# Feed-forward up stage of a two-block transformer kernel: weights as the stationary operand, tokens as the moving one

## The chip, the cores and the metric

The kernel runs on one core of a Trainium2 chip (trn2). The metric is the device time of one execution in microseconds; lower is better. TensorE multiplies (page names PE for matmuls, PEld for the loads of its stationary operand), VectorE (DVE) and ScalarE (ACT) do the elementwise work, SyncE (SP) starts the loads of weights, and GpSimd (POOL) starts a few other transfers. A matmul `matmul(out, lhsT, rhs)` loads `lhsT` into the array (at most 128 x 128) and streams the columns of `rhs` past it (at most 512); the result lands in PSUM, with the columns of `lhsT` as partitions.

## The reference

Two transformer blocks on 256 tokens of width 2048, all in fp32. The part that matters is the feed-forward part at the end of the second block:

```python
h2 = rms_norm_2(x, norm_ffn_pre[l])
up_g, up_v = jnp.split(jnp.einsum('bsd,df->bsf', h2, w_ffn_up[l]), 2, axis=-1)
act = jax.nn.gelu(causal_dwconv3(up_g, conv_ffn_w[l]) + conv_ffn_b[l], approximate=True) * up_v
ffn_out = jnp.einsum('bsf,fd->bsd', act, w_ffn_down[l])
x = x + rms_norm_2(ffn_out, norm_ffn_post[l])

def causal_dwconv3(u, w):          # along the tokens, one weight triple per feature
    return up[:, :s] * w[0] + up[:, 1:s + 1] * w[1] + up[:, 2:] * w[2]
```

`w_ffn_up` is 2048 x 11264 (5632 features of gate, 5632 of value), `w_ffn_down` is 5632 x 2048. The division by the root mean square of a token is one factor per token, and it is applied behind the matmul, to gate and value.

## The kernel before

**One stream of weights.** The program is a sequence of phases (`plan()`), and every phase is a stream of chunks of weights: two k-tiles of 128 rows by 512 columns, 512 KB. SyncE loads a chunk into a ring `raw` of four slots, ScalarE rounds it to fp32r (`hi`), VectorE subtracts to get the rest (`lo = raw - hi`), and TensorE forms each product from three matmuls, `hi*xl`, `hi*xh` and `lo*xh`, where `xh` and `xl` are the same two parts of the activations, already feature-major (features on partitions). ScalarE and VectorE convert three chunks ahead of the one that TensorE is on (`LEAD`); ScalarE's conversion of chunk c + 3 waits until chunk c - 1 has been multiplied, and SyncE's load into a slot waits for `lo` of the chunk that was in it.

**Chunk.** In `chunk()` the activations are the stationary operand: `ah[:, ks, tok]` is 128 features by 128 tokens, and 512 columns of weights stream past. Two k-tiles, two halves of the tokens and three terms make 12 matmuls of 512 columns. The result is token-major (tokens on partitions), 128 x 512 in each of two PSUM banks `acc[pair][t]`. A block of 512 output columns takes eight chunks; gate (block 0, pair 0) and value (block 1, pair 1) of the same 512 features make a pass of 16 chunks.

**Passes.** `ffn_first` is one pass, with the transposes of the activations among its first chunks and the sums for the token factor `rnf` (128 x 2, one column per half of the tokens) in steps 3 to 7; `ffn_up` is a loop of ten; the last pass's elementwise work runs during the first chunks of `ffn_down`. "Step j" of an engine is what it does around chunk j of a pass: VectorE and ScalarE first convert chunk j + 3, then run the side work of the step.

**Side work of a pass, in the next one.** ScalarE evacuates both accumulators with the factor of the token (`ffn_ev`, steps 7 and 15, into `f_g` and `f_v`). TensorE transposes them in groups of four, gate behind chunks 0 and 1, value behind chunks 4 and 5 (`ffn`, into `tp`). VectorE convolves out of PSUM along the tokens (`ffn_conv`, steps 1 and 2, 4 of `tensor_scalar` and 8 of `scalar_tensor_tensor`), ScalarE applies GELU (`ffn_act`, steps 3 and 4), VectorE multiplies by the value (`ffn_mul`, step 6), and the result is split into `fh` and `fl` (`ffn_hi`, `ffn_lo`), the stationary operand of `ffn_down`. The order on each engine is the order in which the code is written; semaphores join the engines (`lo_ready`, `chunk_done`, `acc_free`, and the named steps of a `Stage`).

Of the kernel before, what the change touches and what calls it, by code (L numbers as in the profile page):

```python
# [163 lines left out]
def two_blocks(  # L164
# [152 lines left out]
    f_g = at("f_g", F_W, [T, NB])  # L317
    f_v = at("f_v", F_W + 4096, [T, NB])
# [81 lines left out]
    for n in range(len(LEVELS) + 1):  # L400
# [3 lines left out]
        if n > 0:  # L404
# [9 lines left out]
    ffs = Stage(sem, "ffs", pe=["g0", "g1", "v0", "v1"], act=["ev", "gelu0", "gelu1", "h"],  # L414
                dve=[f"{k}" for c in range(4) for k in (f"c{c}", f"b{c}1", f"b{c}2")] + ["y", "l"])
# [221 lines left out]
    def _(pe):  # L637
# [26 lines left out]
        def stream(side, ready=None):  # L664
            def body(ph, i):
                for j, pos in enumerate(positions(ph)):
                    if ready:
                        ready(i, j)
                    chunk(ph, i, j, pos)
                    side(i, j)  # L670
            return body
# [18 lines left out]
        def stepwise(st, src, ready, side):  # L690
# [12 lines left out]
            return stream(ahead, have)  # L703
# [325 lines left out]
        def ffn_side(i, j):  # L1029
            if j in (0, 1):  # L1030
                ffn(i, j, j)
            if j in (4, 5):
                ffn(i, j, j - 2)

        run(pe, "ffn_first", stepwise(x2_split, lambda t, c: x2[:, t, c:c + P], lambda n: post1.after("dve", f"x{n // 2}"), nothing))
        run(pe, "ffn_up", stream(ffn_side))
        end_phase(pe, "ffn_up", wait=False)

        def down_first(i, j):
            ffn_side(FT // 4 - 1, j)  # L1040
# [4 lines left out]
        run(pe, "ffn_down", stream(nothing), first=stream(down_first, down_ready))  # L1045
# [3 lines left out]
    def _(act):  # L1049
# [447 lines left out]
        def ffn_up(first, ph):  # L1497
            def side(i, j):
                if not first:
                    x2_scales(i, j)  # L1500
                    x2_hi(i, j)
                if first and j in (3, 4):
                    ffn_act(i, j - 3)
                if first and j == 8:
                    ffn_hi(i)
                if j == 7:
                    ffn_ev(i, 0, ph)
                if j == 15:
                    ffn_ev(i, 1, ph)
                    act.drain().then_inc(*ffs.mark("act", "ev"))  # L1510
            return side

        def ffn_act(i, h):
            act.wait_ge(*ffs.after("dve", f"b{2 * h + 1}2", i))
# [9 lines left out]
        run(act, "ffn_first", stream(ffn_up(0, phases["ffn_first"])))  # L1524
        act.wait_ge(out_x2, 16)
        run(act, "ffn_up", stream(ffn_up(1, phases["ffn_up"])))
# [4 lines left out]
        def down_first(i, j):  # L1531
            if j in (3, 4):
                ffn_act(FT // 4 - 1, j - 3)
            if j == 8:
# [12 lines left out]
    def _(dve):  # L1547
# [545 lines left out]
        def ffn_conv(i, h):  # L2093

            dve.wait_ge(*ffs.after("pe", f"g{h}", i))
            for c in (2 * h, 2 * h + 1):
                w = lambda k: vcol[:, V_FW[k][0], bass.ds(i * 4 + (V_FW[k][1] + c), 1)]
                u = tp[h][:, (c % 2) * S:(c % 2 + 1) * S]
                v.tensor_scalar(f_c[:, c], u, w(2), None, ALU.mult).then_inc(*ffs.mark("dve", f"c{c}"))
                dve.wait_ge(*ffs.after("dve", f"c{c}", i))  # L2100
                for back in (1, 2):
                    v.scalar_tensor_tensor(f_c[:, c, back:S], u[:, 0:S - back], w(2 - back), f_c[:, c, back:S],
                                           ALU.mult, ALU.add).then_inc(*ffs.mark("dve", f"b{c}{back}"))
                    dve.wait_ge(*ffs.after("dve", f"b{c}{back}", i))

        def ffn_mul(i):
            dve.wait_ge(*ffs.after("act", "gelu1", i))
# [6 lines left out]
        def ffn_lo(i):  # L2114
            dve.wait_ge(*ffs.after("act", "h", i))
            k = bass.ds(i * 4, 4)
# [16 lines left out]
        def down_side(i, j):  # L2133
            if i == 0:
                ffn_side(FT // 4 - 1, j)
# [31 lines left out]
```

## Time and profile before

| | us |
|---|---|
| median of 3 runs (lowest to highest) | 2629.25 (2628.07 to 2629.6) |
| span of the profiled execution | 2625.2 |
| TensorE, matmuls | 2575.0 busy |
| TensorE, weight loads | 2123.9 busy |
| VectorE | 1482.2 busy |
| ScalarE | 1372.7 busy |
| up stage, one pass of `ffn_up` | 45.45 |

The span of the profiled execution is 4.05 us shorter than the median of the runs. A matmul's record begins when it starts and ends when its results are modelled to have landed, so records overlap: what a stream costs is read from start to start. `acc<-hi,xl` reads as: written to `acc`, moving operand `hi`, stationary operand `xl`; a weight load has the name of its matmul. In a form such as 128*12 128x256 the stationary operand has 12 columns and the moving one 256. The granted clock is 1.00 at 2.4 GHz and 0.50 at 1.2 GHz.

### The profile page before, as it was taken

To read this page: it belongs to the slowest core of one execution; us is meant where nothing else is said; L and a number is where in the kernel's file an instruction comes from. 1 tells how busy PE (TensorE), PEld (TensorE's weight loads), DVE (VectorE), ACT (ScalarE), POOL (GpSimd) and SP (SyncE) were. 2 spreads that over 40 slices of the span, in tenths; PEclk is the share of its full clock that TensorE was granted. 3 is DMA by queue.
4 is the path that set the end of the run, shared out by engine and by line. 5 is a ranking of instruction groups with operands and counts; after the bars stand their busy time and mean duration, and the time that the engine had idled before them with its cause. 6 is when DMAs were issued, how large, how long until landed. Compare 5 with 4: busy or idle time off the path is not lost.

```text
span 2625.2 us, 34962 instructions
## 1 busy us (share of the span) xinstructions
PE 2575.0 (98%) x11926; PEld 2123.9 (81%) x11926; DVE 1482.2 (56%) x1959; ACT 1372.7 (52%) x1925; POOL 9.0 (0%) x17
## 2 busy tenths in 40 slices
PE   7999999999999999999999999999999999999998
PEld 6788788788878888888888888878788888888886
DVE  4455555555556544445477776555556565665444
ACT  5454655555445544454576665444555455554443
POOL 0000000000000000000000000000000000000000
PEclk9999999999999999999999999999999999999999
DMA  7555565556665666655555555666556656566564
GB/s 259 166 162 168 152 193 164 156 173 179 209 215 181 212 192 192 192 169 176 160 161 169 166 169 163 192 198 218 183 179 190 189 178 192 169 198 221 196 198 148
DMA packets 242763, 482.18 MB, mean 184 GB/s; under 512 B 15138, under 2 KB 15440, under 8 KB 240496
## 3 DMA queue, kind: packets, MB, share of 16 engines
q1 hardware_dynamic: 240240, 462.52, 57.7%
q0 software_dynamic: 2432, 18.46, 2.0%
q8 instruction: 56, 0.92, 0.1%
q14 instruction: 35, 0.29, 0.0%
HBM read 474.62 MB, written 6.30 MB: 183 GB/s over the span
## 4 chain that ended last, share of the span: by engine, by line
PE 96%; ACT 2%; DVE 1%; issue 1%; DMA 0%; DVEq 0%; ACTq 0%; SPq 0%
PE acc L639 89%; PE sc L639 3%; PE tp L643 3%; ACT L1051 0%; ACT hi L1051 0%; DVE lo L1552 0%; DMA x_in<-in_x 0%; DVE x2b L2070 0%; ACT sc L1051 0%; PE sc L643 0%; DVE ssh L1722 0%; ACT b_sq L1051 0%; DVE ol L1575 0%; DVE xl L1573 0%; DVE mem_in L1597 0%
## 5 line engine op out<-in xcount | busy, mean ns | idle before, releaser
L1552 DVE TENSOR_TENSOR lo<-raw,hi 128x1024 fp32r<-128x1024 f32 (+1 forms) x896 | 1066.5, 1195 | 940.1 <-ACT hi L1051 932.0
L1051 ACT ACTIVATE hi<-raw 128x1024 fp32r<-128x1024 f32 (+1 forms) x896 | 924.1, 1036 | 845.6 <-PE acc L639 793.9
L639 PE MATMUL acc<-hi,xl 128*128 128x512 f32 x2368 | 946.8, 400 | 9.5 <-DVE lo L1552 5.3
L639 PE MATMUL acc<-lo,xh 128*128 128x512 f32 x2368 | 926.6, 391 | 0.0
L639 PE MATMUL acc<-hi,xh 128*128 128x512 f32 x2368 | 924.6, 390 | 0.0
L639 PEld LDWEIGHTS acc<-hi,xl 128*128 128x128 f32 x2368 | 446.5, 189 | 106.3 <-issue 13.4
L639 PEld LDWEIGHTS acc<-lo,xh 128*128 128x128 f32 x2368 | 445.9, 188 | 96.4
L639 PEld LDWEIGHTS acc<-hi,xh 128*128 128x128 f32 x2368 | 446.9, 189 | 87.5
L639 PE MATMUL acc<-hi,ol 128*128 128x512 f32 x640 | 256.8, 401 | 5.5 <-DVE ol L1575 5.5
L639 PE MATMUL acc<-lo,oh 128*128 128x512 f32 x640 | 250.5, 391 | 0.0
L639 PE MATMUL acc<-hi,oh 128*128 128x512 f32 x640 | 249.8, 390 | 0.0
L639 PEld LDWEIGHTS acc<-hi,ol 128*128 128x128 f32 x640 | 120.7, 189 | 28.8 <-DVE ol L1575 6.0
L639 PEld LDWEIGHTS acc<-lo,oh 128*128 128x128 f32 x640 | 120.4, 188 | 26.4
L639 PEld LDWEIGHTS acc<-hi,oh 128*128 128x128 f32 x640 | 120.9, 189 | 23.2
L639 PE MATMUL acc<-hi,fl 128*128 128x512 f32 x352 | 137.4, 390 | 0.3 <-issue 0.3
L639 PE MATMUL acc<-lo,fh 128*128 128x512 f32 x352 | 137.0, 389 | 0.0
L639 PE MATMUL acc<-hi,fh 128*128 128x512 f32 x352 | 137.0, 389 | 0.0
L1051 ACT ACT_TABLE_LOAD x85 | 109.1, 1283 | 31.7 <-PE tp L643 10.8
L639 PEld LDWEIGHTS acc<-hi,fl 128*128 128x128 f32 x352 | 66.1, 188 | 14.3 <-issue 0.7
L639 PEld LDWEIGHTS acc<-lo,fh 128*128 128x128 f32 x352 | 66.1, 188 | 13.9
L639 PEld LDWEIGHTS acc<-hi,fh 128*128 128x128 f32 x352 | 66.1, 188 | 13.5
L639 PE MATMUL acc<-hi,m2l 128*128 128x512 f32 x128 | 50.7, 396 | 0.3 <-issue 0.3
(301 smaller groups left out, 1478.5 us busy)
## 6 DMA issues: line engine op xcount, KB each, us to landing
raw<-in_w_in SPq DMA_DIRECT2D x416, 512.0 KB, 3.9
raw<-in_w_ffn_up SPq DMA_DIRECT2D x176, 512.0 KB, 4.4
raw<-in_w_ffn_down SPq DMA_DIRECT2D x80, 512.0 KB, 4.7
raw<-in_w_out SPq DMA_DIRECT2D x64, 512.0 KB, 4.4
raw<-in_w_mem_kv SPq DMA_DIRECT2D x48, 512.0 KB, 4.0
raw<-in_w_branch SPq DMA_DIRECT2D x48, 512.0 KB, 4.1
raw<-in_w_branch_a SPq DMA_DIRECT2D x8, 512.0 KB, 4.8
raw<-in_w_branch_b SPq DMA_DIRECT2D x8, 512.0 KB, 4.8
```

Of the source, the lines that this page charges most:

```text
L639: return nc.tensor.matmul(o, lhsT, rhs, start=start, stop=stop)
L643: return nc.tensor.transpose(o, in_, ident[0:k, :])
L1051: return nc.scalar.activation(o, in_, func, **kw)
L1552: v.tensor_tensor(lo[:, slot, 0:size], raw[:, slot, 0:size], hi[:, slot, 0:size].bitcast(F32), ALU.subtract).then_inc(lo_ready, 1)
```

## The change

In `ffn_first` and `ffn_up`, TensorE runs a new `chunk_by_feature`: 128 columns of weights are the stationary operand, all 256 tokens the moving one. Gate and value land feature-major, as the convolution and `ffn_down` want them, and the transposes go. The token factor is then a factor per column: VectorE makes two diagonal matrices from `rnf`, TensorE multiplies them by a matrix of ones, and the result, `f_r`, holds the factor of every token on every partition. VectorE reads the accumulators itself: `ffn_gate` scales the gate from PSUM in step 8 of the same pass, the convolution follows in steps 9 and 10, GELU in 10 and 11, `ffn_scale` multiplies the GELU by the value's factor in step 12, and `ffn_mul` multiplies by the value from PSUM in step 0 of the next pass. ScalarE's `ffn_ev` goes.

```diff
-    f_g = at("f_g", F_W, [T, NB])
-    f_v = at("f_v", F_W + 4096, [T, NB])
+    f_g = at("f_g", F_W, [4, S])
+    f_r = at("f_r", F_W + 4096, [S])
+    f_diag = at("f_diag", F_W + 5120, [T, P])
...
+        def chunk_by_feature(ph, i, j, pos):
...
+            for kk in range(size):
+                ks = place(k0 + kk)
+                for m in range(4):
+                    feat = slice(m * P, (m + 1) * P)
+                    o = acc[pair][m // 2][:, (m % 2) * S:(m % 2 + 1) * S]
+                    end = last and kk == size - 1
+                    opens = k0 + kk == 0 and m % 2 == 0
+                    nc.tensor.matmul(o, hi[:, slot, kk, feat], al[:, ks], start=opens, stop=False, skip_group_check=True)
+                    nc.tensor.matmul(o, hi[:, slot, kk, feat], ah[:, ks], start=False, stop=False, skip_group_check=True)
+                    ins = nc.tensor.matmul(o, lo[:, slot, kk, feat], ah[:, ks], start=False, stop=end, skip_group_check=True)
+            ins.then_inc(chunk_done, 1)
...
-        def ffn(i, at_, step):
-
-            st, n = ("g", f_g) if step < 2 else ("v", f_v)
-            h = step % 2
-            pe.wait_ge(*ffs.after("act", "ev", i))
-            if step >= 2:
-                pe.wait_ge(*ffs.after("dve", f"b{2 * h + 1}2", i))
-            for c in range(2):
+        def first_side(i, j):
+            if j == 8:
+                pe.wait_ge(*ffr.after("dve", "d"))
                 for t in range(T):
-                    ins = tr(tp[h][:, c * S + t * P:c * S + (t + 1) * P], n[:, t, (2 * h + c) * P:(2 * h + c + 1) * P])
-            ins.then_inc(*ffs.mark("pe", f"{st}{h}"))
...
+                    ins = mm(sc[1][:, t * P:(t + 1) * P], kc[:, K_ONE:K_ONE + P], f_diag[:, t])
+                ins.then_inc(*ffr.mark("pe", "r"))
...
-        run(pe, "ffn_up", stream(ffn_side))
+        run(pe, "ffn_up", stream(nothing, one=chunk_by_feature))
...
-        def ffn_ev(i, blk, ph):
-
-            act.wait_ge(chunk_done, ph.chunk(i, KT // 2 * (blk + 1) - 1) + 1)
-            for t in range(T):
-                go((f_g, f_v)[blk][:, t], acc[blk][t][:], ACT.Identity, scale=rnf[:, t:t + 1]).then_inc(acc_free[blk], 1)
...
+        def ffn_side(i, j):
+            if j == 1:
+                ffn_hi(i)
+            if j in (10, 11):
+                ffn_act(i + 1, j - 10)
...
+            if j == 7:
+                dve.wait_ge(*x2_norm.after("dve", "r"))
+                for t in range(T):
+                    ins = v.tensor_scalar(f_diag[:, t], ident, rnf[:, t:t + 1], None, ALU.mult)
+                ins.then_inc(*ffr.mark("dve", "d"))
...
+        def ffn_gate(ph, i, it):
+
+            dve.wait_ge(chunk_done, ph.chunk(i, KT // 2 - 1) + 1)
             for h in range(2):
-                dve.wait_ge(*ffs.after("pe", f"v{h}", i))
+                v.tensor_tensor(f_g[:, 2 * h:2 * h + 2], acc[0][h][:].rearrange("p (a b) -> p a b", a=2), by_token(2),
+                                ALU.mult).then_inc(acc_free[0], 1)
+            dve.drain().then_inc(*ffs.mark("dve", "g0"))
+            dve.wait_ge(*ffs.after("dve", "g0", it))
...
+        def ffn_scale(it):
+            dve.wait_ge(*ffs.after("act", "gelu1", it))
+            v.tensor_tensor(f_a[:], f_a[:], by_token(4), ALU.mult).then_inc(*ffs.mark("dve", "s"))
...
+        def ffn_mul(before, it):
+
+            dve.wait_ge(chunk_done, before + 1)
+            dve.wait_ge(*ffs.after("dve", "s", it))
+            for h in range(2):
                 part = f_a[:, 2 * h:2 * h + 2].rearrange("p a b -> p (a b)")
-                ins = v.tensor_tensor(part, part, tp[h][:], ALU.mult)
-            ins.then_inc(*ffs.mark("dve", "y"))
...
+                v.tensor_tensor(part, part, acc[1][h][:], ALU.mult).then_inc(acc_free[1], 1)
+            dve.drain().then_inc(*ffs.mark("dve", "y"))
...
         def ffn_side(i, j):
-            if j in (1, 2):
-                ffn_conv(i, j - 1)
-            if j == 6:
-                ffn_mul(i)
-            if j == 9:
+            ph = phases["ffn_up"]
+            if j == 0:
+                ffn_mul(ph.chunk(i, -1), i)
+            if j == 2:
                 ffn_lo(i)
+            if j == 8:
+                ffn_gate(ph, i, i + 1)
+            if j in (9, 10):
+                ffn_conv(i + 1, j - 9)
+            if j == 12:
+                ffn_scale(i + 1)
```

In the loop's body TensorE's queue had 208 matmuls (192 and 16 transposes) and now has 384; each is an entry for the weight load and one for the matmul, and with registers and the branch that makes 438 instructions before and 787 after.

TensorE before, in the loop of the up stage, the end of chunk 0 and the first group of transposes (`kc` holds the identity):

```order
L639 MATMUL acc00<-hi_50,xh_52 128x512
L639 MATMUL acc00<-lo_51,xh_52 128x512
L639 MATMUL acc01<-hi_50,xl_53 128x512
L639 MATMUL acc01<-hi_50,xh_52 128x512
L639 MATMUL acc01<-lo_51,xh_52 128x512
L1021 ISA
L643 MATMUL tp0<-kc_60,f_g_157 128x128 x4
```

TensorE after, in the same chunk, a k-tile's four groups of three, two per PSUM bank:

```order
L683 MATMUL acc01<-xh_52,hi_50 128x256
L684 MATMUL acc01<-xh_52,lo_51 128x256
L682 MATMUL acc00<-xl_53,hi_50 128x256
L683 MATMUL acc00<-xh_52,hi_50 128x256
L684 MATMUL acc00<-xh_52,lo_51 128x256
L682 MATMUL acc00<-xl_53,hi_50 128x256
L683 MATMUL acc00<-xh_52,hi_50 128x256
```

The transposes behind the chunk are gone, each matmul has half the columns, and operands have changed sides: the first name behind the arrow is the moving one.

VectorE before, the start of side work in step 1 of the loop, behind the `lo` of that step:

```order
L1552 TENSOR_TENSOR lo<-raw,hi 128x1024
L2095 ISA
L2099 ISA
L2099 TENSOR_SCALAR f_c<-tp,vcol 128x256
L2100 ISA
L2102 ISA
L2102 SCALAR_TENSOR_TENSOR f_c<-tp,vcol,f_c 128x255
```

VectorE after, steps 8 and 9 of the loop:

```order
L1550 TENSOR_TENSOR lo<-raw,hi 128x1024
L2112 TENSOR_TENSOR f_g<-acc,f_r 128x512 x2
L2115 ISA
L1549 REGISTER_ALU
L1550 TENSOR_TENSOR lo<-raw,hi 128x1024
L2122 ISA
L2122 TENSOR_SCALAR f_c<-f_g,vcol 128x256
```

The convolution has moved from steps 1 and 2 of the next pass to steps 9 and 10 of the same one, reads `f_g` in SBUF instead of `tp` in PSUM, and has the scaling out of the accumulators ahead of it.

## Rows read from the trace of the kernel before

**Rows 1.** The page: busy time by engine, and the chain that ended last
```profile
PE 2575.0 (98%) x11926; PEld 2123.9 (81%) x11926; DVE 1482.2 (56%) x1959; ACT 1372.7 (52%) x1925; POOL 9.0 (0%) x17
...
PE 96%; ACT 2%; DVE 1%; issue 1%; DMA 0%; DVEq 0%; ACTq 0%; SPq 0%
PE acc L639 89%; PE sc L639 3%; PE tp L643 3%; ACT L1051 0%; ACT hi L1051 0%; DVE lo L1552 0%; DMA x_in<-in_x 0%; DVE x2b L2070 0%; ACT sc L1051 0%; PE sc L643 0%; DVE ssh L1722 0%; ACT b_sq L1051 0%; DVE ol L1575 0%; DVE xl L1573 0%; DVE mem_in L1597 0%
```
**Rows 2.** One pass: length; busy of PE, PEld, DVE, ACT, POOL; clock, DMA share, GB/s
```profile
1957.45:2002.90 45.45, 45.45 (x210) 37.60 (x209) 27.29 (x32) 24.29 (x27) 0.00 (x0) 1.00 0.61 185
```
**Rows 3.** Groups of instructions, 1912 to 2366: count, busy us, mean ns, idle before, releasers
```profile
L1552 DVE TENSOR_TENSOR lo<-raw,hi 128x1024 fp32r<-128x1024 f32 x160 | 193.4, 1224 | 165.7 <-ACT hi L1051 162.8
L1051 ACT ACTIVATE hi<-raw 128x1024 fp32r<-128x1024 f32 x160 | 168.3, 1058 | 155.3 <-PE acc L639 155.2
...
L2102 DVE SCALAR_TENSOR_TENSOR f_c<-tp,vcol,f_c 128x255 f32<-128x255 f32 x80 | 38.6, 482 | 12.9 <-DVE f_c L2099 2.7 <-DVE f_c L2102 0.2
...
L1051 ACT ACTIVATE f_a<-f_c,vcol 128x256 f32<-128x256 f32 x40 | 18.2, 502 | 17.6 <-DVE f_c L2102 17.5
L2111 DVE TENSOR_TENSOR f_a<-f_a,tp 128x512 f32<-128x512 f32 x20 | 12.8, 681 | 0.0
...
L2117 DVE TENSOR_TENSOR fl<-f_a,fh 128x1024 f32 x10 | 12.2, 1219 | 0.0
```
**Rows 4.** TensorE in order of time, chunk 8 of ffn_first: start us, us, instruction
```profile
1894.06 0.39 PE L639 MATMUL acc<-hi,xl 128*128 128x512 f32 x1
...
1896.78 0.39 PE L639 MATMUL acc<-hi,xl 128*128 128x512 f32 x1
```
**Rows 5.** Tiles `f_g` and `f_v`: ns min/median/max, first and last start us
```profile
L643 PE MATMUL tp<-kc,f_g x88: 270/272/273, 1918.5 to 2377.2; 128*128 128x128 f32 x88
L1051 ACT ACTIVATE f_g<-acc,rnf x22: 681/686/690, 1894.3 to 2349.4; 128x512 f32<-128x512 f32 x22
...
L643 PE MATMUL tp<-kc,f_v x88: 270/272/273, 1930.4 to 2389.0; 128*128 128x128 f32 x88
```
**Rows 6.** TensorE in order of time, around a group of transposes
```profile
1918.31 0.39 PE L639 MATMUL acc<-lo,xh 128*128 128x512 f32 x1
1918.54 0.60 PE L643 MATMUL tp<-kc,f_g 128*128 128x128 f32 x4
...
1919.21 0.40 PE L639 MATMUL acc<-hi,xh 128*128 128x512 f32 x1
...
1919.91 0.39 PE L639 MATMUL acc<-hi,xh 128*128 128x512 f32 x1
```
**Rows 7.** Tile `rnf` in `ffn_first`, its last write
```profile
L1613 DVE RECIPROCAL rnf<-rnf x1: 158/158/158, 1894.1 to 1894.1; 128x2 f32<-128x2 f32 x1
```
**Rows 8.** TensorE: 256 fp32r columns past 12 columns of weights; last, their window
```profile
270.13 0.28 PE L639 MATMUL sc<-xh,wf_lo 128*12 128x256 f32 x1
...
271.88 0.28 PE L639 MATMUL sc<-xh,wf_lo 128*12 128x256 f32 x1
...
275.39 0.28 PE L639 MATMUL sc<-xh,wf_hi 128*12 128x256 f32 x1
...
271.90:275.40 3.50, 3.50 (x34) 2.81 (x32) 1.23 (x1) 1.43 (x5) 0.00 (x0) 1.00 0.79 187
```
**Rows 9.** Weight loads in order of time, merged, ahead of fp32 matmuls of 128 and 256 columns
```profile
544.24 0.86 PEld L639 LDWEIGHTS sc<-mk,c_pt 128*128 128x128 f32 x7
...
1152.83 1.48 PEld L639 LDWEIGHTS sc<-d_kt,d_qt 128*128 128x128 f32 x7
```
**Rows 10.** ScalarE and VectorE in order of time, conversion of one chunk
```profile
1996.04 1.06 ACT L1051 ACTIVATE hi<-raw 128x1024 fp32r<-128x1024 f32 x1 [1.66 <-PE acc L639]
...
1997.14 1.23 DVE L1552 TENSOR_TENSOR lo<-raw,hi 128x1024 fp32r<-128x1024 f32 x1 [1.49 <-ACT hi L1051]
```
**Rows 11.** DMA queues (packets, MB, share): 1912 to 1957 first, then 1957.5 to 2366
```profile
q1 hardware_dynamic: 4335, 8.35, 59.4%
q8 instruction: 2, 0.03, 0.3%
...
q1 hardware_dynamic: 39124, 75.42, 60.4%
...
raw<-in_w_ffn_up SPq DMA_DIRECT2D x139, 512.0 KB, 4.4
```

More of the change, by code:

```diff
@@ L413, in two_blocks @@
     post1 = Stage(sem, "post1", act=["rt"], dve=["w0", "w1", "w2", "ms", "e", "w3", "r", "x0", "x1", "x2", "x3"])
[L414 to L415 removed]
+    ffr = Stage(sem, "ffr", pe=["r"], dve=["d", "r"])
+    ffs = Stage(sem, "ffs", act=["gelu0", "gelu1", "h"],
+                dve=["g0"] + [f"{k}{h}" for h in range(2) for k in ("c", "b", "d")] + ["s", "y", "l"])
     post2 = Stage(sem, "post2", act=["rt"], dve=["w0", "w1", "w2", "ms", "e", "w3", "r", "x0", "x1", "x2", "x3"])
@@ L662, in chunk, with stream @@
             ins.then_inc(chunk_done, 1)
-        def stream(side, ready=None):
+        def chunk_by_feature(ph, i, j, pos):
+            blk, k0, size, last = pos
+            pair = blk % 2
+            slot = (ph.c0 + j) % RING
+            ah, al, place = stationary(ph.name, blk)
+            if k0 == 0 and not (isinstance(i, int) and ph.use(i, blk) == 0):
+                pe.wait_ge(acc_free[pair], 2 * ph.use(i, blk))
+            pe.wait_ge(lo_ready, ph.chunk(i, j) + 1)
+            for kk in range(size):
[9 more added lines that the diff above has]
+            ins.then_inc(chunk_done, 1)
+        def stream(side, ready=None, one=chunk):
             def body(ph, i):
@@ L668, in body @@
                         ready(i, j)
-                    chunk(ph, i, j, pos)
+                    one(ph, i, j, pos)
                     side(i, j)
@@ L688, in norm_split, with stepwise @@
             split(st, src, st.after("dve", "n1"), n)
-        def stepwise(st, src, ready, side):
+        def stepwise(st, src, ready, side, one=chunk):
             for n in range(2):
@@ L702, in have @@
                     pe.wait_ge(*st.after("dve", f"l{j}"))
-            return stream(ahead, have)
+            return stream(ahead, have, one)
         pe.wait_ge(in_first, 16 * 2)
@@ L1044, in down_ready @@
                 pe.wait_ge(*ffs.after("dve", "l", FT // 4 - 1))
-        run(pe, "ffn_down", stream(nothing), first=stream(down_first, down_ready))
+        run(pe, "ffn_down", stream(nothing), first=stream(nothing, down_ready))
     @block_ctx.scalar
@@ L1489, in _, with first_side @@
         end_phase(act, "out_2", wait=False)
-        def ffn_ev(i, blk, ph):
-            act.wait_ge(chunk_done, ph.chunk(i, KT // 2 * (blk + 1) - 1) + 1)
-            for t in range(T):
-                go((f_g, f_v)[blk][:, t], acc[blk][t][:], ACT.Identity, scale=rnf[:, t:t + 1]).then_inc(acc_free[blk], 1)
[L1497 to L1511, printed above, removed]
+        def first_side(i, j):
+            x2_scales(i, j)
+            x2_hi(i, j)
+            if j in (11, 12):
+                ffn_act(0, j - 11)
+        def ffn_side(i, j):
[3 more added lines that the diff above has]
+                ffn_act(i + 1, j - 10)
         def ffn_act(i, h):
-            act.wait_ge(*ffs.after("dve", f"b{2 * h + 1}2", i))
+            act.wait_ge(*ffs.after("dve", f"d{h}", i))
             for c in (2 * h, 2 * h + 1):
@@ L1521, in ffn_hi @@
             go(fh[:, bass.ds(i * 4, 4)], f_a[:]).then_inc(*ffs.mark("act", "h"))
-        run(act, "ffn_first", stream(ffn_up(0, phases["ffn_first"])))
+        run(act, "ffn_first", stream(first_side))
         act.wait_ge(out_x2, 16)
-        run(act, "ffn_up", stream(ffn_up(1, phases["ffn_up"])))
+        run(act, "ffn_up", stream(ffn_side))
         end_phase(act, "ffn_up")
@@ L2091, in first_side @@
             x2_scales(i, j)
[L2093 to L2104, printed above, removed]
@@ new lines, in first_side, with by_token @@
+            if j == 9:
+                dve.wait_ge(*ffr.after("pe", "r"))
+                v.tensor_copy(f_r[:], sc[1][:, 0:S]).then_inc(*ffr.mark("dve", "r"))
+                dve.wait_ge(*ffr.after("dve", "r"))
+                ffn_gate(phases["ffn_first"], 0, 0)
+            if j in (10, 11):
+                ffn_conv(0, j - 10)
+            if j == 13:
+                ffn_scale(0)
+        def by_token(n):
+            return f_r[:].unsqueeze(1).to_broadcast([P, n, S])
+        def ffn_gate(ph, i, it):
+            dve.wait_ge(chunk_done, ph.chunk(i, KT // 2 - 1) + 1)
+            for h in range(2):
+                v.tensor_tensor(f_g[:, 2 * h:2 * h + 2], acc[0][h][:].rearrange("p (a b) -> p a b", a=2), by_token(2),
+                                ALU.mult).then_inc(acc_free[0], 1)
+            dve.drain().then_inc(*ffs.mark("dve", "g0"))
+            dve.wait_ge(*ffs.after("dve", "g0", it))
@@ new lines, in ffn_conv @@
+        def ffn_conv(it, h):
+            w = lambda c, k: vcol[:, V_FW[k][0], bass.ds(it * 4 + (V_FW[k][1] + c), 1)]
+            two = (2 * h, 2 * h + 1)
+            for c in two:
+                ins = v.tensor_scalar(f_c[:, c], f_g[:, c], w(c, 2), None, ALU.mult)
+            ins.then_inc(*ffs.mark("dve", f"c{h}"))
+            for back, was, step in ((1, "c", "b"), (2, "b", "d")):
+                dve.wait_ge(*ffs.after("dve", f"{was}{h}", it))
+                for c in two:
+                    ins = v.scalar_tensor_tensor(f_c[:, c, back:S], f_g[:, c, 0:S - back], w(c, 2 - back), f_c[:, c, back:S],
+                                                 ALU.mult, ALU.add)
+                ins.then_inc(*ffs.mark("dve", f"{step}{h}"))
@@ L2133, in down_side @@
         def down_side(i, j):
-            if i == 0:
-                ffn_side(FT // 4 - 1, j)
+            if (i, j) == (0, 0):
+                ffn_mul(ph.chunk(0, -1), FT // 4 - 1)
+            if (i, j) == (0, 2):
+                ffn_lo(FT // 4 - 1)
             if (i, j) in ((0, 26), (1, 2), (1, 26)):
```

22 lines of the change are left out of this document (6 added, 16 removed).

## The prediction, made before the changed kernel ran

> **What bounds the kernel now.** I read the page first: TensorE is busy 98% of the span and carries 96% of the chain that ended last, almost all of it matmuls into `acc` [rows 1]. So only what shortens or lengthens TensorE's stream counts, or what makes it wait. Then one pass of the up stage: in 45.45 us TensorE is busy for all of them at a granted clock of 1.00, the 2.4 GHz level, while VectorE works 27.3 us and ScalarE 24.3 us [rows 2]. Both have idle time ahead of their work on weights: in ten passes VectorE waits 165.7 us ahead of `lo` for ScalarE, and ScalarE 155.3 us ahead of `hi` for TensorE [rows 3]. TensorE is the bound, and its helpers have slack.
>
> **What a clean chunk costs.** In a stretch without transposes, from the matmul at 1894.06 to the one at 1896.78, 12 matmuls of 512 columns take 2.72 us, 226.7 ns from start to start [rows 4]. The 390 ns of a single one is latency, which the next one overlaps. A pass has 16 chunks of 12, so 192 x 0.2267 = 43.52 us. The pass takes 45.45 us: from the first evacuation of gates at 1894.3 to the last at 2349.4, second of its pair and so 0.6 late, ten passes go by in 454.5 us [rows 5].
>
> **What the change removes on TensorE.** 88 transposes of `f_g` and as many of `f_v`, in groups of four, 4 groups in each of 11 passes [rows 5]. Read one group: the last matmul ahead of it starts at 1918.31, the second behind it at 1919.21, so 0.90 us hold two matmuls' worth of stream (0.453) and 0.445 us that are the group's [rows 6]. The three steps from 1919.21 to 1919.91 are slower than clean ones by 0.02 us together. Four groups make 1.9 us, and 45.45 - 43.52 = 1.93 us says the same from the other side. All of it lies on the path: 11 x 1.93 = **21.2 us gained**.
>
> **What it adds on TensorE.** Two fp32 matmuls for the row `f_r`, once. Plain fp32 is run as two passes, so four entries of the kind of a transpose group: 0.5 us. They wait for `f_diag`, made by VectorE in step 7. `rnf` is final at 1894.1 + 0.16, and TensorE asks for the diagonals behind chunk 8, at 1896.78 [rows 4, 7]. Two small operations fit in 2.5 us, so I take no wait.
>
> **What it exchanges, the term that decides.** Each matmul of 512 columns becomes two of 256, with the weights as stationary operand: 384 instead of 192 in a pass, and as many weight loads. The columns streamed are the same. A weight load must now hide behind 256 columns, and the trace has no 256-column fp32r matmul with a full 128-column load. I bound one by four neighbours:
> - 256 fp32r columns with a load of 12 columns: from 271.88 to 275.39 are 31 steps, 113.3 ns each, and the clock is at 1.00 there [rows 8]. That is half of 226.7 to a tenth of a nanosecond. Since the 512-column matmul had a load of 128 columns and this one of 12, neither the number of instructions nor the size of the load shows in the time. Sum by it: no change.
> - Loads of 128 columns back to back behind short fp32 matmuls: seven loads in 0.86 us, the last 0.19 long, so (0.86 - 0.19)/6 = 112 ns from one to the next [rows 9]. A full load is done in 112 ns, just under 113.3.
> - fp32 matmuls of 256 columns in two passes, 512 half-steps each: (1.48 - 0.19)/6 = 215 ns for a computed 213.3 [rows 9]. Full loads hide entirely behind them; some 2 ns could be a fixed part of each matmul.
> - The first 15 steps of the 256-column row, from 270.13 to 271.88, took 117 ns each [rows 8]. I do not know why.
>
> Least is 0 (the same columns cannot stream faster than the row), and most, if the whole 13.4 ns above 213.3 in a 512-column step belonged to the instruction, is 106.7 + 13.4 = 120 ns. I take 113.3, because the nearest row by data type and width has it and the load fits by 1 ns. **Exchange: 0, bounds 0 to 4224 x 6.7 ns = +28 us**, 4224 being 11 x 384.
>
> The Trainium skill, TensorE: Matmul & The Clock Gate, section Back-to-back issue gap, speaks against the change: warm matmuls are N/2.4 plus about 2.5 ns apart, so a split costs 2.5 ns each time. By that the 2112 additional matmuls would cost 5.3 us and the sum would be 5.3 us worse. The fp32 rows agree with such a part, the fp32r rows at 113.3 and 226.7 do not.
>
> **What moves on VectorE and ScalarE.** ScalarE loses four evacuations of 0.69 us per pass [rows 5], and by the order of instructions the loads of an activation table too. VectorE gets two products from PSUM, like the 0.68 us of `f_a<-f_a,tp`, and one of 1024 columns, like the 1.22 us of `fl`: 2.6 us more, 29.9 of 43.5 [rows 3]. The busy time is harmless; the order needs a look, because the next `lo` stands behind each wait. Chunk c's `lo` is due 3 chunks (8.16 us) after the start of chunk c-3; normally it is ready 2.3 us after it (`hi` 1996.04, `lo` done 1998.37) [rows 10]. The waits for `acc` in steps 0 and 8 come behind a `lo` whose `hi` itself waited for the same chunk, so they cost nothing. The convolution of steps 9 and 10 is 12 operations; I take 0.48 us for each, as eight of them took before [rows 3]. `lo` of step 9 ends at 2.4 us into chunk 9, the first half at 5.4, `lo` of step 10 at 6.6, the second half at 9.6, two more `lo` by 12.1. The last of them, of chunk 15, is then 12.1 - 3 x 2.72 = 3.9 us into chunk 12 if only VectorE is counted; its `hi` stands behind the second GELU on ScalarE (9.6 + 1.0 + 1.1 = 11.7, so `lo` at 12.9, 4.8 us into chunk 12) [rows 3]. Due is 8.16. Cover: over 3 us. Without it each further microsecond per pass costs 11. A `raw` slot falls free with that `lo` and is filled in a median 4.4 us [rows 11]: 9.2 us into chunk 12, which is before its own `hi` at 10.9. I cost these edits at nothing.
>
> **Sum.** 2625.2 - 21.2 + 0.5 = 2604.5 us by the profiled execution. The median of the runs is 4.05 us above that span, so **2608.5 us**, 0.8% faster. It breaks even at 113.3 + 20.7 us/4224 = 118.2 ns a step.
>
> **Rivals.**
> - *A fixed part in each matmul.* 2.1 ns, as the fp32 rows allow: 2112 x 2.1 = 4.4 us, **2613 us**. For it: rows 9. Against it: rows 8. The skill's rule of 2.5 ns above is this rival, a microsecond worse.
> - *The weight load shows through.* 112 ns is so near to 113.3 that a handshake or two reads of SBUF at once could set the pace. At the 117 ns of the first steps in rows 8: 4224 x 3.6 ns = 15 us, **2624 us**. For it: those steps, and that the load is now hidden by nothing but 1 ns. Against it: the 31 steps behind them.
> - *Slower: the excess belongs to the load, not to the columns.* 120 ns a step costs 28 us: **2637 us**. It decides from 118.2 ns on. For it: every fp32r matmul with a 128-column load is 13.4 ns over its 512/2.4. Against it: the 12-column rows pay exactly half of it for half the columns.
> - *Slower: the loop no longer stays with the engine.* The body grows from 438 to 787 instructions on TensorE's queue. In the first pass two pieces of code of 16 KB are fetched, and in the nine that follow none [rows 11]. So 438 instructions, touching three pieces of 256, are kept across the branch. If 787 are not, each of 9 branches waits up to a transfer's 4.4 us: up to 40 us, **2648 us** at most. The Trainium skill, Runtime: NRT & Kernel Launch, section Instruction fetch mechanics, says that a taken branch to code outside a two-page window stalls for the fetch. By that rule the loop before would have fetched too, and rows 11 show that it did not; the same section gives TensorE room for 2048 instructions, which no run here shows.
> - *A new wait.* VectorE's convolution takes over 3 us longer than reckoned and TensorE waits at chunk 15. The gain is gone at 1.9 us per pass: **about 2620 to 2630 us**.
>
> **How the numbers follow.** Forecast (no change in the exchange) 0.50; fixed part 0.15; load shows through (115 to 118 ns) 0.13; load pays 120 ns 0.12; loop not kept 0.05; new wait 0.05. The range runs from 2604, since the runs of before spread over 1.5 us and what a removed group trails behind it may reach further than I counted, to 2627, which takes in the first three cases and the mild half of a new wait: 0.80. A measurement of this kernel tells 0.2% (5.3 us) from no change. Faster by more (under 2624.0): 0.50 + 0.15 + 0.11 + 0.02 = 0.78. Within it: 0.02 + 0.02 + 0.01 = 0.05. Slower: 0.17.
>
> **What would show it.** One pass of the up stage at 43.5 us and TensorE without idle time in it; steps of 113 ns between 256-column matmuls, 112 or less from load to load where they queue; clock 1.00; no instruction packets between the first pass and the last; `lo` of chunk 15 ready 3 us early. It is wrong if the steps are 117 ns or more, if weight loads lie end to end with matmuls behind them, or if TensorE idles before chunk 0, 15 or 16 of a pass.

## The result, and the profile after

The changed kernel takes 2633.9 us in the median of 19 runs (2629.74 to 2636.69), beside 2629.14 for the kernel before in the median of as many (2623.64 to 2630.69). The ratio is 1.0023, with a 95% interval of 1.0016 to 1.0030. A second comparison gave 2633.34 against 2627.01, 1.0030 [1.0018, 1.0042]. So the kernel got slower, by 0.2 to 0.3%, where 0.8% faster was forecast, and the time lies 7 us above the end of the range.

The page of the changed kernel, its busy times, the chain, and two of the new groups:

```profile
PE 2579.6 (98%) x13866; PEld 2217.2 (84%) x13866; DVE 1497.3 (57%) x1995; ACT 1324.2 (50%) x1862; POOL 9.0 (0%) x17
...
PE 96%; ACT 2%; DVE 1%; issue 1%; DMA 0%; DVEq 0%; ACTq 0%; SPq 0%
...
L682 PE MATMUL acc<-xl,hi 128*128 128x256 f32 x1408 | 400.3, 284 | 1.0 <-DVE xl L1571 1.0
...
L682 PEld LDWEIGHTS acc<-xl,hi 128*128 128x128 f32 x1408 | 271.4, 193 | 1.4 <-DVE xl L1571 1.4
```

TensorE has 1940 more matmuls (13866 against 11926 in [rows 1]): 2112 from the split and 4 for the row `f_r`, less 176 transposes. It is still the bound, with the same 98% and 96%. The only new names in the chain are those of the new matmuls.

One pass of the up stage, in the columns of [rows 2], an interval between two taken branches of the loop:

```profile
2006.20:2052.28 46.08, 46.08 (x386) 46.08 (x386) 28.57 (x34) 19.49 (x22) 0.00 (x0) 1.00 0.62 182
```

It is 46.08 us, where 45.45 stood before and 43.5 was forecast. The clock is 1.00, so nothing was lost there. What is new is the third number: the weight loads fill the whole pass (before 37.60 of 45.45), as the prediction listed among its signs of being wrong. A load's record is 192 ns long and the next load starts 120 ns behind it, so this number alone doesn't say that the loads set the pace. TensorE in order of time, inside that stage:

```profile
1998.22 0.28 PE L684 MATMUL acc<-xh,lo 128*128 128x256 f32 x1
1998.34 0.28 PE L682 MATMUL acc<-xl,hi 128*128 128x256 f32 x1
1998.46 0.28 PE L683 MATMUL acc<-xh,hi 128*128 128x256 f32 x1
1998.58 0.28 PE L684 MATMUL acc<-xh,lo 128*128 128x256 f32 x1
```

Each step is 0.12 us. From 2004 to 2054 us 416 matmuls start, each 120 ns behind the one before it, to the nanosecond, where 113.3 was forecast. 384 x 0.120 = 46.08: the step accounts for the pass, and there is no other time in it. What the pass gained by losing its transposes (1.93 us) is less than what 384 steps lost (384 x 6.7 ns = 2.56 us), and the difference of 0.63 us comes 11 times, 6.9 us. The eleventh time is `ffn_first`, whose matmuls are slower too, against the transposes that are gone from the start of `ffn_down`. The matmuls for `f_r` add 0.44 us once. The two profiled spans differ by 4.4 us, not by 7.3. Of the other 2.9 us, 2.5 arose before the changed stage, since TensorE starts its first matmul in `ffn_first` at 1863.99 us here and at 1866.45 in the kernel before. The rest is in the first six chunks of `ffn_first`.

All the waits that the profile of the changed kernel shows from 1960 to 2370 us (who waited for what, us in total, times, longest us):

```profile
ACT hi L1061 <- PE acc L684: 211.1, 125, 1.8
DVE lo L1550 <- ACT hi L1061: 151.0, 116, 1.7
ACT f_a L1061 <- DVE f_c L2127: 26.4, 18, 1.8
```

TensorE is not among those that wait. The loss is therefore in the pace of its own stream.

### The profile page after: what moved, and what is told of

It reads as the page before. It is cut to its first block, busy times and chain, and to the rows that moved or that the text cites. A ratio compares the mean times of both kernels' runs of the same rounds, so it can differ in the third digit from the quotient of the medians.

```text
span 2629.6 us, 38693 instructions
## 1 busy us (share of the span) xinstructions
PE 2579.6 (98%) x13866; PEld 2217.2 (84%) x13866; DVE 1497.3 (57%) x1995; ACT 1324.2 (50%) x1862; POOL 9.0 (0%) x17
## 4 chain that ended last, share of the span: by engine, by line
PE 96%; ACT 2%; DVE 1%; issue 1%; DMA 0%; DVEq 0%; ACTq 0%; SPq 0%
PE acc L641 71%; PE acc L682 6%; PE acc L684 6%; PE acc L683 6%; PE sc L641 3%; PE tp L645 2%; ACT L1061 0%; ACT hi L1061 0%; DVE lo L1550 0%; DMA x_in<-in_x 0%; DVE x2b L2068 0%; ACT sc L1061 0%; PE sc L645 0%; DVE ssh L1720 0%; ACT b_sq L1061 0%
## 5 line engine op out<-in xcount | busy, mean ns | idle before, releaser
L641 PE MATMUL acc<-hi,xl 128*128 128x512 f32 x1664 | 666.7, 401 | 8.5 <-DVE lo L1550 5.3
L641 PE MATMUL acc<-lo,xh 128*128 128x512 f32 x1664 | 650.6, 391 | 0.0
L641 PE MATMUL acc<-hi,xh 128*128 128x512 f32 x1664 | 649.2, 390 | 0.0
L682 PE MATMUL acc<-xl,hi 128*128 128x256 f32 x1408 | 400.3, 284 | 1.0 <-DVE xl L1571 1.0
L684 PE MATMUL acc<-xh,lo 128*128 128x256 f32 x1408 | 399.5, 284 | 0.0
L683 PE MATMUL acc<-xh,hi 128*128 128x256 f32 x1408 | 399.5, 284 | 0.0
L641 PEld LDWEIGHTS acc<-hi,xh 128*128 128x128 f32 x1664 | 313.9, 189 | 60.8
L682 PEld LDWEIGHTS acc<-xl,hi 128*128 128x128 f32 x1408 | 271.4, 193 | 1.4 <-DVE xl L1571 1.4
L683 PEld LDWEIGHTS acc<-xh,hi 128*128 128x128 f32 x1408 | 271.4, 193 | 0.0
L684 PEld LDWEIGHTS acc<-xh,lo 128*128 128x128 f32 x1408 | 271.4, 193 | 0.0
```

Of the source, the lines that this page charges most:

```text
L641: return nc.tensor.matmul(o, lhsT, rhs, start=start, stop=stop)
L682: nc.tensor.matmul(o, hi[:, slot, kk, feat], al[:, ks], start=opens, stop=False, skip_group_check=True)
L683: nc.tensor.matmul(o, hi[:, slot, kk, feat], ah[:, ks], start=False, stop=False, skip_group_check=True)
L684: ins = nc.tensor.matmul(o, lo[:, slot, kk, feat], ah[:, ks], start=False, stop=end, skip_group_check=True)
```

## The experiments

The order is that of what they decide: first the two halves of the change apart, then the disputed step by itself, then versions that use what was learned.

**The transposes gone, the matmuls as before.** The changed kernel with token-major matmuls of 512 columns in both up stages:

```diff
-                                       first_side, chunk_by_feature))
-        run(pe, "ffn_up", stream(nothing, one=chunk_by_feature))
+                                       first_side))
+        run(pe, "ffn_up", stream(nothing))
```

> The changed kernel with its elementwise work and without transposes, but the up stage multiplied as before (activations stationary, 512 columns of weights moving), so what lands in the accumulators is token-major and the output is not the reference's. It is the removal alone. If the transposes' cost was read rightly, a pass takes 43.5 us instead of 45.45 and the time is 21 us under the kernel before: ratio 0.992. If the new work on VectorE delays TensorE, or the transposes were partly hidden, less than that.

Measured: 2607.15 us beside 2626.94, ratio 0.9921 [0.9905, 0.9938]. That is 20.8 us gained by the ratio, 19.8 between the medians. Its pass:

```profile
2005.00:2048.52 43.52, 43.52 (x194) 36.05 (x193) 28.57 (x34) 19.55 (x22) 0.00 (x0) 1.00 0.62 192
```

43.52 us is 192 x 226.7 ns and nothing beside it. The new work of VectorE and ScalarE is all in this kernel, and it costs nothing. The term of 21.2 us for the removal holds: ten passes are 1.93 us shorter each.

**The split alone.** The kernel before, transposes and all, with `chunk_by_feature` put in for its matmuls:

```diff
-        run(pe, "ffn_up", stream(ffn_side))
+        run(pe, "ffn_up", stream(ffn_side, one=chunk_by_feature))
```

and the same in `ffn_first`.

> The kernel before, with the up stage's matmuls exchanged for the 256-column ones (weights stationary) and everything else left, transposes and evacuations too; gate and value are then in the wrong layout, so the output is not the reference's. It is the exchange alone. At 120 ns a step instead of 113.3: 11 passes x 384 x 6.7 ns = 28 us slower, ratio 1.011. If the 120 ns came from something else in the changed kernel (VectorE reading the accumulators, for one), the steps here are 113.3 ns and the ratio is 1.000.

Measured: 2653.59 us beside 2626.94, ratio 1.0102 [1.0085, 1.0119]. That is 26.8 us lost by the ratio, 26.7 between the medians. TensorE in order of time:

```profile
1999.77 0.28 PE L682 MATMUL acc<-xh,lo 128*128 128x256 f32 x1
1999.89 0.28 PE L680 MATMUL acc<-xl,hi 128*128 128x256 f32 x1
2000.01 0.28 PE L681 MATMUL acc<-xh,hi 128*128 128x256 f32 x1
```

Again 120 ns, without VectorE reading the accumulators. The two halves, -20.8 and +26.8 by their ratios, add up to +6.0 us. The change as a whole costs 6.0 and 7.9 us by the ratios of its two comparisons, 4.8 and 6.3 between the medians. So the failing term is the exchange, and the other terms are right. What remained was why a step takes 120 ns, since two rivals (the load shows through; a fixed part in each matmul) and the slower one (the excess belongs to the load) could all be stretched to it.

**The step by itself.** A kernel of its own with groups of 48 matmuls in a row, each group with one shape and one PSUM bank, stationary tiles taken in turn, and nothing else running:

```diff
+        for k in range(N): mm(ps[1][:, 0:384], wr[k % 2][:, 0:128], xr[:, 0:384], start=True, stop=True)
+        for k in range(N): mm(ps[3][:, 0:256], wr[k % 2][:, 0:128], xr[:, 0:256], start=True, stop=True)
+        for k in range(N): mm(ps[3][0:12, 0:256], wr[k % 2][:, 0:12], xr[:, 0:256], start=True, stop=True)
```

> No part of the reference: groups of 48 matmuls, stationary operand of m columns, moving one of n, one after the other on an idle chip. Theory A: each weight load of 128 columns costs the stream 13.3 ns whatever streams behind it, one of 12 columns 6.7 ns. Then m=128: n=512 227, 384 173.3, 320 146.7, 256 120, and 192 and 128 at the load's own pace, about 112; m=12: 256 113.3, 512 220; pairs of 512 and 256: 347. Theory B: columns of fp32r stream at 16/17 of the clock, and a load behind such a stream takes 120 ns. Then m=128: n=384 170, 320 141.7, 256, 192 and 128 all 120; m=12: 256 113.3, 512 226.7; m=64, n=256 113.3. fp32 of 256 columns is 215 in both; bfloat16 is not in the trace: A says 227 and 120 again.

TensorE in order of time, each group merged into one row (start, length of the whole group, shapes of load and matmul, count):

```profile
27.97 11.04 PE L59 MATMUL ps<-xr,wr 128*128 128x512 f32 x48
38.85 8.51 PE L60 MATMUL ps<-xr,wr 128*128 128x384 f32 x48
47.20 7.19 PE L61 MATMUL ps<-xr,wr 128*128 128x320 f32 x48
54.23 5.92 PE L62 MATMUL ps<-xr,wr 128*128 128x256 f32 x48
...
65.74 5.50 PE L64 MATMUL ps<-xr,wr 128*128 128x192 f32 x48
71.08 5.50 PE L65 MATMUL ps<-xr,wr 128*128 128x128 f32 x48
...
98.36 5.60 PE L69 MATMUL ps<-xr,wr 128*12 128x256 f32 x48
103.80 11.26 PE L70 MATMUL ps<-xr,wr 128*12 128x512 f32 x48
114.90 20.88 PE L71 MATMUL ps<-xf,wf 128*128 128x256 f32 x96
...
156.69 5.40 PE L74 MATMUL ps<-xb,wb 128*128 128x256 bf16 x48
```

A group's length less its last matmul's duration, over 47, is the step: for 256 columns (5.92 - 0.28)/47 = 120.0 ns. In the same way 512 columns give 226.7, 384 give 173.3, 320 give 146.7. (Where the first few steps of a group are uneven, the number is that of the settled ones behind them; for 384 columns the whole group would give 173.9.) The granted clock is 1.00 throughout. Taking away columns / 2.4 leaves 13.3 ns **every time**, at 256 as at 512, as long as the load has 128 columns. At 192 and at 128 columns the step stays at 111.7: there the load sets the pace, and the 112 ns from [rows 9] was right. The same stationary tile each time instead of two in turn (the next row of that kernel) gives 120.0 as well. The row with a load of 12 columns, on which the forecast rested, is there too: 113.3, and loads of 32 and 64 columns give the same to half a nanosecond. But 12 columns of load with 512 of matmul take 231 ns, more than a full load does, so a small load isn't simply cheaper.

Other data types have a far smaller fixed part. bf16 takes 109.2 ns for 256 columns (and 215.8 for 512, 55.8 for 128), where 106.7 are the columns alone. The 48 fp32 matmuls of 256 columns are 96 entries in the row above, and each entry takes 215.8 ns, 2.5 more than twice its 256 columns. By the Trainium skill, TensorE: Matmul & The Clock Gate, section Back-to-back issue gap, steps of N columns are N/2.4 plus about 2.5 ns. The trace agrees with that for bf16. It doesn't for fp32r, which has 13.3, and an fp32 entry has the 2.5 only over twice its columns.

Of the two theories on record the full-load rows fit the first, 13.3 ns for each load of 128 columns. It missed bf16 (227 and 120 expected) and the 12-column load behind 512 columns (220 expected). Every matmul here has a load of its own, so a fixed part in each matmul and one in each load look the same until the load's size changes.

**Loads of other sizes.** At 256 columns the full load gave 120.0 and small ones 113.3. If the size of the load were the cause, the step should follow it. The same kernel with other shapes:

```diff
+        for k in range(N): mm(ps[1][0:112, 0:256], wr[k % 2][:, 0:112], xr[:, 0:256], start=True, stop=True)
+        for k in range(N): mm(ps[3][0:80, 0:256], wr[k % 2][:, 0:80], xr[:, 0:256], start=True, stop=True)
+        for k in range(N): mm(ps[2][0:12, 0:384], wr[k % 2][:, 0:12], xr[:, 0:384], start=True, stop=True)
```

> No part of the reference: groups of 48 matmuls of fp32r, stationary operand of m columns, moving one of n. From the first table the price of a load is 13.3 ns for 128 columns and 6.7 for 64, 32 and 12, when n is 256. If it goes by started halves of 64 columns, m=72 to 112 cost 13.3 (120 ns at n=256) and 64 costs 6.7; if in proportion, 96 columns cost 10 to 12. At n=384 and 320: m=128 13.3 over the columns; m=64, 32, 12: 166.7 and 140 if the price is the load's, else the erratic 230 of n=512 shows here too. Pairs of 512 and 256 in separate banks: 347. 64 rows instead of 128 at m=128, n=256: 120 if the price goes by columns of weights, less if by bytes of the whole load.

```profile
27.66 5.92 PE L59 MATMUL ps<-xr,wr 128*128 128x256 f32 x48
33.41 5.61 PE L60 MATMUL ps<-xr,wr 128*112 128x256 f32 x48
38.85 5.73 PE L61 MATMUL ps<-xr,wr 128*96 128x256 f32 x48
44.42 5.62 PE L62 MATMUL ps<-xr,wr 128*80 128x256 f32 x48
...
69.32 8.48 PE L66 MATMUL ps<-xr,wr 128*64 128x384 f32 x48
...
85.97 8.54 PE L68 MATMUL ps<-xr,wr 128*12 128x384 f32 x48
```

Loads of 112, 96, 80, 72 and 64 columns give steps of 113.4, 116.1, 113.3, 116.7 and 113.4 ns. There is no order among them, neither the halves nor the proportion that was expected, but all lie below the 120.0 of the full load. At 384 columns a smaller load saves nothing: 175.0 for 96 columns of load, 173.4 for 64, 173.3 for 32, 175.0 for 12, beside 173.3 for a full one. So "the excess belongs to the load" is no rule for all widths. At 256 columns, the width of the changed kernel, 3.3 to 6.7 of the 13.3 ns do go with the full load in this kernel.

**Widths around 256.** The same again in steps of 16 columns, with full loads and with loads of 12:

```diff
+        for k in range(N): mm(ps[4][0:128, 0:272], wr[k % 2][:, 0:128], xr[:, 0:272], start=True, stop=True)
+        for k in range(N): mm(ps[5][0:12, 0:256], wr[k % 2][:, 0:12], xr[:, 0:256], start=True, stop=True)
+        for k in range(N): mm(ps[6][0:12, 0:272], wr[k % 2][:, 0:12], xr[:, 0:272], start=True, stop=True)
```

> No part of the reference: groups of 48 fp32r matmuls, m columns stationary, n moving. Theory C, by the tables so far: steps come in units of 6.67 ns (16 columns), a stream pays one or two units over its own, and a full load, whose own pace is 111.7 ns, just misses the 113.3 that 256 columns would take. Then m=128: n=208 to 240 about 111.7 to 113.3, 256 120, 272 120 to 126.7, the same as m=12 from 272 or 288 on; m=120 or 124 at n=256: between 113.3 and 120. Theory A (a price on each full load) wants m=128 over m=12 by 6.7 ns at every n. Runs: 512 and 256 by turns 353 a pair, in runs of 2, 4, 8 falling to 346.7.

| columns | 208 | 224 | 240 | 256 | 272 | 288 | 304 | 320 |
|---|---|---|---|---|---|---|---|---|
| columns / 2.4, ns | 86.7 | 93.3 | 100.0 | 106.7 | 113.3 | 120.0 | 126.7 | 133.3 |
| step, load of 128 | 111.6 | 111.6 | 111.7 | 120.0 | 125.3 | 131.7 | 137.7 | 146.7 |
| step, load of 12 | | | 111.1 | 117.8 | 124.4 | 131.2 | 140.0 | 146.7 |

```profile
43.74 5.91 PE L62 MATMUL ps<-xr,wr 128*128 128x256 f32 x48
49.49 6.18 PE L63 MATMUL ps<-xr,wr 128*128 128x272 f32 x48
...
75.48 5.80 PE L67 MATMUL ps<-xr,wr 128*120 128x256 f32 x48
81.12 5.91 PE L68 MATMUL ps<-xr,wr 128*124 128x256 f32 x48
...
98.23 5.81 PE L71 MATMUL ps<-xr,wr 128*12 128x256 f32 x48
103.88 6.14 PE L72 MATMUL ps<-xr,wr 128*12 128x272 f32 x48
```

From 256 columns on, a step in this kernel is the columns and 11 to 13.3 ns, with either load. At 272 the small load costs what the full one does, to a nanosecond. The load of 12 columns with 256 took 117.8 ns here and 113.3 in the first kernel of steps, for the same shape. So the row that the forecast took as its nearest neighbour stands for one width, and it isn't even stable there; [rows 8] shows both of its paces, 117 ns for the first 15 steps and 113.3 for the 31 behind them.

At 256 columns the two rows above add the loads between 112 and 128 columns: 117.3 ns for 120 columns and 120.0 for 124. That is where the theory on record put them, by which a full load, at its own pace of 111.7, just misses the 113.3 that the columns would take. What isn't separated is how much of the 120 ns at 256 columns is the fixed part and how much the load: by the kernel before this one the load's share is up to 6.7 ns, by this one, against the 12-column load, 2.2. With the full load of the changed kernel all three kernels give 120.0, and the price doesn't depend on the answer.

**Fewer, wider matmuls, feature-major.** If each fp32r matmul with a full load pays 13.3 ns, the changed kernel can win some back by joining two of the three terms: `hi` meets `xh` and `xl`, both with the same stationary tile, so one matmul of 512 columns can do for two of 256. Its two halves land side by side in a whole PSUM bank (the four banks of `acc` and `sc` or `tp` take a chunk's four feature tiles), `lo` times `xh` is added to the second half, ScalarE copies the first half out, and VectorE adds the second to it. Only the loop `ffn_up` is changed so; `ffn_first` stays as in the changed kernel:

```diff
+                for m in range(4):
...
+                    if ks == 0:
+                        nc.tensor.matmul(wide[pair][m][:], hi[:, slot, kk, feat], both, start=True, stop=False, skip_group_check=True)
+                    ins = nc.tensor.matmul(wide[pair][m][:, S:], lo[:, slot, kk, feat], xh[:, ks], start=False, stop=False, skip_group_check=True)
+                    if ks:
+                        ins = nc.tensor.matmul(wide[pair][m][:], hi[:, slot, kk, feat], both, start=False, stop=end, skip_group_check=True)
```

> The changed kernel, and in ffn_up the two terms that share a stationary operand, hi*xh and hi*xl, are one matmul of 512 columns into a whole bank; lo*xh stays at 256 columns, ScalarE copies one half of each bank and VectorE adds the other. 256 loads in a pass instead of 384, the same columns. If each full load costs 13.3 ns of stream (theory A), a pass takes 128 x (226.7 + 120) = 44.4 us, against 46.1 changed and 45.45 before: 17 us under the changed kernel, 12 us under the one before, ratio 0.995. If the price belongs to columns (theory B) and 120 ns is a floor of the load, the sum is the same 44.4, so this run does not tell the theories apart; it tells whether fewer loads pay in the kernel. If the extra work (3 us a pass on VectorE, 1.5 us on ScalarE) delays TensorE, less.

Measured: 2624.93 us beside 2627.01, ratio 0.9992 [0.9983, 1.0001], level with the kernel before. Its pass:

```profile
2005.56:2050.77 45.21, 45.21 (x259) 39.24 (x257) 31.07 (x41) 21.59 (x29) 0.00 (x0) 1.00 0.63 186
```

The direction is right, 0.87 us less than the changed kernel's 46.08. But a pair of 512 and 256 columns takes 353.2 ns (45.21 us / 128), 6.5 more than 226.7 + 120.0, and the pass misses the 44.4 us expected. TensorE has no wait in it, so the extra work of the other engines isn't what delays it.

**The same, equal widths in runs.** In each k-tile four matmuls of one width and then four of the other, with the order reversed from one k-tile to the next, so that up to eight of a width stand in a row:

```diff
+                for term in ("hi", "lo") if ks % 2 == 0 else ("lo", "hi"):
+                    for m in range(4):
```

> e4 with the order of matmuls changed: eight of 512 columns in a row, then eight of 256, instead of one by one. In e4 a pair took 353 ns instead of 346.7, and in the second table a mixture of widths was as uneven. If the turn from one width to the other costs, runs of eight bring the pair near 346.7 and a pass from 45.2 to 44.4 or 44.5 us: 7 us under e4, ratio 0.996 to the kernel before. If the 353 belong to the joined operand or to the bank written, nothing changes: 0.999.

Measured: 2620.83 us beside 2626.8, ratio 0.9974 [0.9963, 0.9984]. Its pass:

```profile
2004.72:2049.41 44.69, 44.69 (x258) 39.33 (x257) 31.00 (x41) 21.59 (x29) 0.00 (x0) 1.00 0.64 188
```

A pair takes 349.1 ns now (44.69 / 128), still 2.4 over the sum. This one beats both kernels: by its ratio 6.8 us under the one before (6.0 between the medians), and by the ratios 13 to 15 us under the changed one, whose ratios are 1.0023 and 1.0030. The traces say the same: ten passes at 44.69 instead of 45.45 are 7.6 us, less 1.1 us for what stays as in the changed kernel (`ffn_first` 2.56 slower, `f_r` 0.44, and the last pass's transposes, 1.93, gone from the start of `ffn_down`).

**The changed kernel again**, beside the first joined one:

> The changed kernel itself, beside the others on the same chip: 4 to 7 us over the kernel before, ratio 1.0023 as measured first.

Measured: 2633.34 us, ratio 1.0030, told above.

## Why the prediction was wrong, step by step

- **What bounds the kernel, and a clean chunk:** right. TensorE has no idle time in the up stage before or after, and without transposes a pass is 43.52 us, as computed.
- **What is removed, 21.2 us:** right, 20.8 measured by the ratio and 19.8 between the medians.
- **What is added, 0.5 us for `f_r`:** right. The diagonals are made at 1892.5 us and used at 1895.2, so there is no wait, and chunk 8 of `ffn_first` with them is 0.44 us longer than its neighbours.
- **What it exchanges: 0 was taken, it was +28 us by the steps** (4224 x 6.7 ns) and 26.8 by the run of the split alone, where a pass with its transposes takes 47.81 us: 46.08 and 1.73 for the transposes, which cost 0.2 less there. This is the step that failed. The forecast set 113.3 ns (a load of 12 columns, 256 of matmul) beside 226.7 (load of 128, 512 of matmul), saw exactly half, and concluded that the 13.3 ns over 512/2.4 are proportional to the columns. That changed two sizes between two rows and read a law out of their ratio. With the full load kept, the 13.3 ns are the same at 256, 320, 384 and 512 columns, so halving the columns pays them twice. The coincidence came from the one width where a smaller load is cheaper: 113.3 is found at 256 columns alone, with loads of up to 112 columns, and not in every program. The upper bound, "if the whole 13.4 ns belonged to the instruction, 120 ns", was the truth; it got 0.12 of the chance because the coincidence to a tenth of a nanosecond looked like evidence.
- **A fixed part in each matmul:** the mechanism that fits every row with a full load, with the wrong size. It was sized at 2.1 ns from plain fp32 matmuls in [rows 9], and another data type didn't carry over: fp32r has 13.3. The 2.5 ns that the prediction took from the Trainium skill would have been off in the same way.
- **The weight load shows through, 117 ns:** its number for the load's own pace was right (111.7), and from 208 to 240 columns the step is the load's. At 256 the step is 8.3 ns above that pace, so the load alone doesn't account for it; that it has a share of up to 6.7 ns isn't excluded, as the rows with smaller loads show.
- **The excess belongs to the load, 2637 us:** its price of 120 ns a step was the measured one. As a mechanism it fails from 272 columns on, where a smaller load saves at most 1 ns, and at 512 columns it costs 3 to 4 more. At 256 it can hold for half of the 13.3 ns and not for all of them.
- **The loop no longer stays with the engine:** didn't happen. DMA queues of the changed kernel (packets, MB, share), 1912 to 1960 us first, then 1960 to 2374:

```profile
q1 hardware_dynamic: 4610, 8.89, 62.7%
q8 instruction: 3, 0.05, 0.4%
...
q1 hardware_dynamic: 39060, 75.30, 62.3%
```

Three pieces of code come in the first pass and none in the nine that follow, whose window has no row for an instruction queue, so 787 instructions are kept across the branch. The Trainium skill, Runtime: NRT & Kernel Launch, section Instruction fetch mechanics, has a taken branch out of a two-page window stall for a fetch. The trace doesn't show that: the matmuls run on at 120 ns across the branch.
- **A new wait on VectorE:** didn't happen, with more room than reckoned. VectorE in order of time:

```profile
2033.53 1.28 DVE L2112 TENSOR_TENSOR f_g<-acc,f_r 128x512 f32<-128x512 f32 x2
2035.27 1.23 DVE L1550 TENSOR_TENSOR lo<-raw,hi 128x1024 fp32r<-128x1024 f32 x1 [0.46 <-ACT hi L1061]
2036.41 0.61 DVE L2122 TENSOR_SCALAR f_c<-f_g,vcol 128x256 f32<-128x256 f32 x2
2037.16 1.90 DVE L2127 SCALAR_TENSOR_TENSOR f_c<-f_g,vcol,f_c 128x255 f32<-128x255 f32 x4
...
2044.80 1.23 DVE L1550 TENSOR_TENSOR lo<-raw,hi 128x1024 fp32r<-128x1024 f32 x1 [0.89 <-ACT hi L1061]
```

Chunk 8 starts at 2031.1 (the `hi` that waits for it begins at 2031.30), so chunk 12 starts 4 x 2.88 later, at 2042.6. The `lo` of chunk 15 is done at 2046.03, 3.4 us into it, due at 8.64: 5.2 us of cover, where over 3 were forecast. One part of the surplus is the `TENSOR_SCALAR` that now reads SBUF: 348 ns, where it took 482 from PSUM before and was forecast at that. VectorE's pass is 28.57 us (29.9 forecast) and ScalarE's 19.49.

With the terms as the runs measured them the sum is 2625.2 - 20.8 + 0.4 + 26.8 = 2631.6 us of span, 2635.7 with the 4.05 us on top, beside 2633.9 measured.

## What to carry to other kernels

Price a matmul stream as columns plus a part for each matmul, and take that part from rows of the same data type and the same size of load; for fp32r with a full load it was 13.3 ns, 6% of a 512-column step and 11% of a 256-column one, so a layout that halves the moving width must save more than that elsewhere. Where a term decides the sign and the trace has no row for it, a neighbour that differs in two sizes proves nothing however neatly it fits; a kernel of 48 equal matmuls settles it in 6 us of TensorE time. Where terms share a stationary operand, try joining them into one wide matmul and keeping equal widths together: here that turned a loss of 0.2 to 0.3% into a gain of 0.3%.

## What the runs showed of the hardware that was not expected

- fp32r matmuls with a full load take 11 to 13.3 ns more than their columns, from 256 to 512 columns; bf16 matmuls and fp32 entries in the same kernel, 2.5. Why is not shown. The steps of 256, 320, 384 and 512 columns stand exactly at 13.3 over the columns, those of 272, 288 and 304 at 12.0, 11.7 and 11.0.
- A load of 12 columns can make things worse: with 512 columns of matmul 231 ns, beside 226.7 for a full load; a load of 64 gives 230. With 256 columns it gives 113.3 or 117.8 in different programs. What decides between them stays open.
- The fixed part is there at the upper clock level only. At the start of `ffn_first` the granted clock is 0.50, the 1.2 GHz level, in both kernels; in the kernel before, TensorE had been busy for 1.97 of the 5.40 us from 1861.0 on. TensorE in order of time, the changed kernel first, then the one before:

```profile
1864.59 0.41 PE L684 MATMUL acc<-xh,lo 128*128 128x256 f32 x1
1864.80 0.41 PE L682 MATMUL acc<-xl,hi 128*128 128x256 f32 x1
1865.01 0.41 PE L683 MATMUL acc<-xh,hi 128*128 128x256 f32 x1
...
1867.47 0.63 PE L639 MATMUL acc<-lo,xh 128*128 128x512 f32 x1
1867.89 0.63 PE L639 MATMUL acc<-hi,xl 128*128 128x512 f32 x1
```

The steps there are 213.3 and 426.7 ns in the mean, 256/1.2 and 512/1.2 and nothing beside them. So halving the columns costs nothing in that stretch, and chunk 0 of `ffn_first` takes 5.99 us in both kernels.

- Turning between widths has a price that depends on something else. In groups of 48 alternating 512 and 256 columns, 47 steps should take 8.20 us (24 x 226.7 + 23 x 120.0). All in one PSUM bank they took 8.29 us in one kernel and 8.22 in another, and with each width in a bank of its own 8.46. Runs of two, four and eight in one bank took 8.25, 8.30 and 8.26, so longer runs gained nothing there, against what was expected. In the joined kernels, whose matmuls go through four banks, pairs were 6.5 and 2.4 ns over the sum. Whether banks, widths or both are the cause wasn't separated.
